# Splitting the weight panels of the latent-attention and grouped-query layers on ScalarE and VectorE instead of GpSimd

## What is computed

```python
def trunk_layer(l, x, cond, ctx):
    mod = (jax.nn.silu(cond) @ w_mod[l] + b_mod[l]).reshape(cond.shape[0], 6, D_MODEL)[:, :, None, :]
    h = rmsnorm(x, g_norm1[l]) * (1.0 + mod[:, 1]) + mod[:, 0]
    out, ctx_tensors = token_mixer(l, h, ctx)      # 0: MLA, 1: differential, 2: GQA, 3: RG-LRU
    x = x + mod[:, 2] * out
    h = rmsnorm(x, g_norm2[l]) * (1.0 + mod[:, 4]) + mod[:, 3]
    x = x + mod[:, 5] * swiglu(h, w_ffn_in[l], w_ffn_out[l])
    return x, ctx_tensors
```

## Time and profile before

| what | value |
|---|---|
| median of 3 runs | 3607.74 us (3607.37 to 3613.88) |
| the profiled execution's own time | 3609.12 us |
| its span, first to last instruction | 3606.8 us |
| mean granted TensorE clock, as a share of full speed | 0.963 |
| instructions | 52935 |

### The profile page before, as it was taken

How to read it: one execution, slowest core, us unless ns; L and a number is a source line. 1 busy time by engine, 2 the same in 40 slices (tenths; PEclk the granted TensorE clock), 3 DMA queues, 4 the chain that set the end, 5 groups by cost and what they waited for, 6 DMA issues and landing times.

```text
span 3606.8 us, 52935 instructions
## 1 busy us (share of the span) xinstructions
PE 3318.1 (92%) x20320; PEld 3011.4 (83%) x20320; DVE 1878.0 (52%) x2728; ACT 1132.7 (31%) x1742; POOL 117.5 (3%) x72
## 2 busy tenths in 40 slices
PE   7979898999998998899999788989999897899999
PEld 2556677999987776789999766779999897899999
DVE  2133346858354666466763544567573688533333
ACT  1334433211125555232111333232111377321111
POOL 0311100000000000000000221000000000000000
PEclk9989999999999999899999899999999999999999
DMA  7300013444221110153532210143432221222222
GB/s 260 109 21 13 18 33 120 145 146 142 74 82 37 42 47 17 47 176 120 177 93 70 57 31 18 35 145 124 162 123 76 62 67 47 59 76 76 76 74 77
DMA packets 421861, 304.11 MB, mean 84 GB/s; under 512 B 12019, under 2 KB 389494, under 8 KB 421622
## 3 DMA queue, kind: packets, MB, share of 16 engines
q1 hardware_dynamic: 411412, 293.23, 26.2%
q10 hardware_dynamic: 10338, 9.41, 0.8%
HBM read 298.49 MB, written 4.10 MB: 84 GB/s over the span
## 4 chain that ended last, share of the span: by engine, by line
PE 83%; DVE 7%; ACT 5%; DVEq 2%; issue 2%; ACTq 1%; DMA 1%; SPq 0%
PE psB L310 29%; PE psA L310 29%; PE psD L310 7%; PE psC L373 3%; PE psA L354 2%; PE psC L326 2%; PE psC L365 2%; PE psB L354 2%; ACT h_hi L1392 1%; PE psA L761 1%; ACT work L1389 1%; PE psB L761 1%; ACTq L1391 1%; ACT work L412 1%; DMA raw<-in_w_ffn_in 1%
## 5 line engine op out<-in xcount | busy, mean ns | idle before, releaser
L1410 ACT ACTIVATE w_hi<-raw 128x1024 fp32r<-128x1024 f32 (+1 forms) x309 | 319.3, 1035 | 1165.2 <-PE psB L310 766.2
L1943 DVE TENSOR_TENSOR w_lo<-raw,w_hi 128x1024 fp32r<-128x1024 f32 (+1 forms) x309 | 367.9, 1192 | 347.8 <-ACT w_hi L1410 347.5
L310 PE MATMUL psA<-h_hi,w_hi 128*128 128x320 f32 x1616 | 384.5, 320 | 72.0 <-DVE h_lo L2014 59.9
L310 PE MATMUL psB<-h_hi,w_hi 128*128 128x320 f32 x1616 | 370.0, 310 | 15.5 <-DVE w_lo L2296 15.5
L310 PE MATMUL psA<-h_lo,w_hi 128*128 128x320 f32 x1616 | 375.4, 314 | 0.0
L310 PE MATMUL psA<-h_hi,w_lo 128*128 128x320 f32 x1616 | 375.1, 314 | 0.0
L310 PE MATMUL psB<-h_lo,w_hi 128*128 128x320 f32 x1616 | 369.2, 310 | 0.0
L310 PE MATMUL psB<-h_hi,w_lo 128*128 128x320 f32 x1616 | 369.1, 310 | 0.0
L310 PEld LDWEIGHTS psA<-h_hi,w_hi 128*128 128x128 f32 x1616 | 273.9, 192 | 91.9 <-issue 43.8
L1973 DVE SCALAR_TENSOR_TENSOR work<-work,silu_c 128x1024 f32<-128x1024 f32 x252 | 312.5, 1281 | 12.4 <-issue 0.9
L310 PEld LDWEIGHTS psB<-h_hi,w_hi 128*128 128x128 f32 x1616 | 271.0, 188 | 17.1 <-DVE w_lo L2296 17.1
(11 more groups left out here) (290 smaller groups left out, 5137.8 us busy)
## 6 DMA issues: line engine op xcount, KB each, us to landing
raw<-in_w_ffn_in SPq DMA_DIRECT2D x176, 512.0 KB, 3.9
work<-in_w_mod SPq DMA_DIRECT2D x144, 512.0 KB, 4.8
raw<-in_w_ffn_out SPq DMA_DIRECT2D x64, 512.0 KB, 3.9
work<-in_w_mod SPq DMA_DIRECT2D x12, 2048.0 KB, 7.9
raw<-in_w_ffn_out SPq DMA_DIRECT2D x32, 384.0 KB, 3.3
raw<-in_diff_w_in SPq DMA_DIRECT2D x24, 512.0 KB, 3.8
raw<-in_lru_w_in SPq DMA_DIRECT2D x16, 512.0 KB, 4.0
raw<-in_gqa_w_in SPq DMA_DIRECT2D x12, 512.0 KB, 3.8
```

Of the source, the lines that this page charges most:

```text
L310: last = nc.tensor.matmul(out[:, b, 0:half], w[slot][:, kt * cols + c0:kt * cols + c0 + P], r[:, o:o + half], start=(kt == 0 and p == 0), ...
L1410: nc.scalar.activation(w_hi[s][:, 0:n], raw[s][:, 0:n], ACT.Copy).then_inc(hi_done, 1)
L1943: nc.vector.tensor_tensor(w_lo[s_][:, 0:n], raw[s_][:, 0:n], w_hi[s_][:, 0:n].bitcast(F32), ALU.subtract).then_inc(split_done, 1)
```

## The change

The four phases are marked dense, so that ScalarE and VectorE split their panels too. GpSimd's block and its semaphore go. The new splits are placed by hand in the programs of ScalarE and VectorE; `per=1` is for `gqa`, where a head takes one panel and the slots alternate. Nothing in TensorE's and SyncE's programs is edited.

```diff
-            add("mla_in", 3, (0, 1), [(KT, P)] * 2)
-            add("mla", HEADS, (0, 1), [(3, 192), (2, 256)])
+            add("mla_in", 3, (0, 1), [(KT, P)] * 2, True)
+            add("mla", HEADS, (0, 1), [(3, 192), (2, 256)], True)
...
-            add("gqa_kv", 2, (0, 1), [(KT, P)] * 2)
-            add("gqa", HEADS // 2, (0, 1), [(KT, P)] * 2)
+            add("gqa_kv", 2, (0, 1), [(KT, P)] * 2, True)
+            add("gqa", HEADS // 2, (0, 1), [(KT, P)] * 2, True)
...
-        @block.gpsimd
-        def _(pool):
...
         @block.scalar
...
+            for j in range(2):
+                high_part("mla_in", 0, j)
             for layer in range(DEPTH):
                 norm(2 * layer)
...
                         acts.mark(evacuate(mla_raw[t], mla_sq[t], psum[t % 2], TH), f"m{t}")
+                        if t < 4:
+                            high_part("mla_in", t // 2 + 1, t % 2)
+                        else:
+                            high_part("mla", 0, t % 2)
...
                         act_pt(act, A, h, 3, m_PT, m_PTp)
+                        if later:
+                            high_part_of_head("mla", n.next(), 0)
                         prep(evv)
                         act_pt(act, A, h, 4, m_PT, m_PTp)
+                        if later:
+                            high_part_of_head("mla", n.next(), 1)
                         prep(values)
...
-                    for step in (evqn, evqr, rsqn, rsqr, evkn, rskn, evv, values):
+                    for step in (evqn, evqr, rsqn, rsqr, evkn, rskn, evv):
                         step(h0)
+                    for j in range(2):
+                        high_part_of_head("mla", Head(0, 1), j)
+                    values(h0)
...
                         acts.mark(evacuate(gk_t[j][:, 0:T], gsq, psA, TH), "evk")
+                        high_part(("gqa_kv", "gqa")[j], 1 - j, 0)
                         g_panel("gqa_kv", j, 1)
                         acts.mark(nc.scalar.activation(halves(gvt, TH), psB[:, :, 0:TH], ACT.Copy), "evv")
+                        high_part(("gqa_kv", "gqa")[j], 1 - j, 1)
...
                         act_pt(act, A, h, 0, g_PT, g_PTp)
+                        if later:
+                            high_part_of_head("gqa", n.next(), 0, 1)
                         act_exp(act, A, h, 2, 1, scale, g_probs, g_stats)
...
-                    projected(f"out{layer}.{ch}", f"in{layer}.{ch + 1}" if ch < 2 else {0: "diff", 2: "lru"}.get(layer))
+                    projected(f"out{layer}.{ch}", f"in{layer}.{ch + 1}" if ch < 2 else {0: "diff", 1: "gqa_kv", 2: "lru"}.get(layer))
...
         @block.vector
...
+            for j in range(2):
+                low_part("mla_in", 0, j)
             for layer in range(DEPTH):
                 norm(2 * layer)
...
                     nc.vector.memset(kr_cache, 0.0).then_inc(kr_cleared, 1)
+                    for t in range(4):
+                        low_part("mla_in", t // 2 + 1, t % 2)
+                    for j in range(2):
+                        low_part("mla", 0, j)
...
                         pv.wait(dve, "pv", h)
                         out.mark(split_head(dve, h.at(T, 0)), "o")
+                        if later:
+                            low_part_of_head("mla", n.next(), 0)
                         if more:
                             probs(n, 1)
+                        if later:
+                            low_part_of_head("mla", n.next(), 1)
...
                         step(h0)
+                    for j in range(2):
+                        low_part_of_head("mla", Head(0, 1), j)
                     largest(h0, 0)
...
                     for j in range(2):
+                        low_part(("gqa_kv", "gqa")[j], 1 - j, 0)
+                        low_part(("gqa_kv", "gqa")[j], 1 - j, 1)
                         acts.wait(dve, "rsk", j)
...
                             kind(h, t)
+                            if later and (kind, t) == (probs, 2):
+                                low_part_of_head("gqa", n.next(), h.k % 2, 1)
...
-                                   f"in{layer}.{ch + 1}" if ch < 2 else {0: "diff", 2: "lru"}.get(layer), mod,
+                                   f"in{layer}.{ch + 1}" if ch < 2 else {0: "diff", 1: "gqa_kv", 2: "lru"}.get(layer), mod,
```

More of the change, by code:

```diff
@@ L1408, in high_part, with high_part_of_head @@
                 act.wait_ge(raw_in[s], i * 16 + 16 * (ph.landed[s] + 1))
-                act.wait_ge(gemm_done, i * ph.n + (ph.first + j + 1 - ph.n))
+                if ph.first or not isinstance(i, int) or i:
+                    act.wait_ge(gemm_done, i * ph.n + (ph.first + j + 1 - ph.n))
                 nc.scalar.activation(w_hi[s][:, 0:n], raw[s][:, 0:n], ACT.Copy).then_inc(hi_done, 1)
-            def high_part_of_head(name, h, j):
+            def high_part_of_head(name, h, j, per=None):
                 ph = phases[name]
-                s, n = ph.slots[j], ph.shape[j][0] * ph.shape[j][1]
-                act.wait_ge(raw_in[s], h.at(16, 16 * (ph.landed[s] + 1)))
-                act.wait_ge(gemm_done, h.at(ph.n, ph.first + j + 1 - ph.n))
+                per = per or ph.n
+                if per == 1:
+                    j = h.k % 2
+                    s, n = ph.slots[j], ph.shape[j][0] * ph.shape[j][1]
+                    act.wait_ge(raw_in[s], h.i * 16 + 16 * (ph.landed[s] + 1 + h.k // 2))
+                    act.wait_ge(gemm_done, h.at(1, ph.first + 1 - ph.n))
+                else:
+                    s, n = ph.slots[j], ph.shape[j][0] * ph.shape[j][1]
+                    act.wait_ge(raw_in[s], h.at(16, 16 * (ph.landed[s] + 1)))
+                    act.wait_ge(gemm_done, h.at(ph.n, ph.first + j + 1 - ph.n))
                 nc.scalar.activation(w_hi[s][:, 0:n], raw[s][:, 0:n], ACT.Copy).then_inc(hi_done, 1)
@@ L1504, in exp, with head @@
                         act_exp(act, A, h, t, 1, scale, m_probs, m_stats)
-                    def head(h, more):
+                    def head(h, more, later=True):
                         n = h.next()
@@ L1537, in _ @@
                     for k in range(2):
-                        head(Head(HEADS // 2 - 1, k), k == 0)
+                        head(Head(HEADS // 2 - 1, k), k == 0, later=False)
                 elif layer == 1:
```

5 lines of the change are left out of this document (2 added, 3 removed).

## The result

The changed kernel takes 3621.91 us (median of 6 runs, 3617.38 to 3628.37) against 3607.60 us for the kernel before (6 runs, 3607.28 to 3613.88): 14.3 us or 0.41% slower, ratio 1.0041 with the 95% interval 1.0029 to 1.0053. The profiled execution took 3624.09 us with a span of 3622.2 us, 15.0 us above the profiled execution of before.

The account below looks back on a forecast made before the run. TensorE, busy 92% of the span, was taken as the bound, so only its waits count. 18.5 + 7.2 + 0.1 - 3.7 - 1.7 - 1.0 + 0.3 = +19.7 us, on the median 3627.4 us; range 3614 to 3638.

Parts of the forecast that it names:

- The stall: Layer 0 head handover: TensorE's gqn waits for the w_lo behind split_head, 3.08 us in six heads, +18.5 us.
- The clock: Layer 0 heads: TensorE runs at half clock behind most of the six stalls, 1.2 us each, +7.2 us.
- rival (a): Layer 0: the stall comes, but the clock does not follow or wins its loss back; +12.5 us, 3620 us, chance 0.22.
- The forecast's own sign: Layer 0: if TensorE waits for w_lo but the head grows by 3.1 us or less, only the clock term is wrong.
- Start of layer 2: Last sum of squares and TensorE's wait shorten without GpSimd's w_lo beside them, as in layer 1; -3.7 us, lower end 2.5.
- Key and value heads: Layer 2, twice: L451 speeds up without GpSimd, less a delay by ScalarE's new w_hi; net 0.8 each, -1.7 us.
- Query heads: Layer 2: L442 falls from 1.05 to about 0.55 us without GpSimd; five heads, -1.0 us.
- some 0.2 us a head reach TensorE: Layer 2 query heads: the part of L442's saving that shortens TensorE's time; five heads, -1.0 us.
- Rival (b): Layer 2 query heads: w_hi before tile 2's exponential delays TensorE, six heads lose 1.06 each, +6.4; 3635 us, chance 0.12.
- Start of the kernel: ScalarE gets two w_hi, 2.1 us, into 1.74 us of idle before the first reciprocal root; +0.3 us.
- Rival (c): Handover in layer 0 costs nothing and only the gains remain, -6.0 us; 3602 us, chance 0.05.
- Rival (d): Whole kernel: the change doesn't do what it says, as if only the idle's place changes; within 5 us of 3608, chance 0.03.

Follow-up runs that it names:

- experiment 1: The changed kernel with the first w_lo of a latent-attention head written before VectorE waits for the head's output; 3598.05 us against 3603.59 for the kernel before.
- experiment 2: The changed kernel with that w_lo before the output only in every second head, leaving three of six stalls; 3606.25 us against 3603.59 for the kernel before.
- experiment 8: The kernel before, all splits on GpSimd, with TensorE also waiting for VectorE's split_head before gqn; 3622.50 us against 3607.01 for the kernel before.
- experiment 9: Kernel 1 with the w_lo of layer 2's query heads put behind split_head; 3606.77 us against 3605.79 for the kernel before.
- kernel 1: The changed kernel with the first latent-attention w_lo before VectorE's wait for the output; 3598.05 us against 3603.59, later 3598.80 against 3605.79, for the kernel before.
- Experiment 7: The kernel before, with GpSimd waiting for the last sum of squares before splitting layer 2's first panels; 3606.49 us against 3607.01 for the kernel before.
- the layer-0 part alone: The change for layer 0 only, GpSimd still splitting layer 2's panels; 3629.95 us against 3607.01 for the kernel before.
- The layer-2 part alone: The change for layer 2 only, GpSimd still splitting layer 0's panels; 3598.02 us against 3607.01 for the kernel before.
- experiment 10: Kernel 1 run once more, unedited, beside the kernel before; 3598.80 us against 3605.79.
- experiment 6: The layer-2 part alone: GpSimd still splits layer 0's panels; 3598.02 us against 3607.01 for the kernel before.

## Why the prediction was right, and by what it missed

The forecast was slower, 3627 us with a range of 3614 to 3638; measured were 3621.9. The mechanism was right, and one term of the sum was much too large. On the forecast's own terms, in the profiled pair, +19.7 was expected and +15.0 came.

- **The stall**: 3.08 us by six heads, 18.5. Measured 18.4, at the six places named. Its parts held to 0.1 us: `split_head` through 2.3 us after the start of `gqn` of before, a `w_lo` of 0.75, a wake-up of 0.05. Experiments 1, 2, 8 and 9 show that this is the cause.
- **The clock**: +7.2 was foretold, and this is the step that failed. The cost of the new half-clock stretches was nearly right, 7.8 us behind five stalls. Left out of the middle value was that the stretches which five of the heads had before would go with the new spacing: -6.7. The text had allowed for it only as an end of the range, a gain of 3. Net +1.1. The outcome is rival (a), which gave 3620 us and 0.22. The forecast's own sign (a head that grows by 3.1 us or less) does not catch it: a head grew from 37.3 to 40.6 us where a new stretch replaced an old one.
  The Trainium skill (TensorE: Matmul & The Clock Gate, Part 1) puts the fall of the clock down to an idle stretch before it. Five of the six stalls agree; behind the third, of 2.82 us, the clock stays full. The stretches of the kernel before agree less well: in the 7.1 us in front of one of them TensorE's longest idle time is 1.70 us. A sum that adds only what a new idle does to the clock is one-sided.
- **Start of layer 2**: -3.7 foretold, -2.6 in the profile after. The wait fell as foretold (5.70 to 3.04 us); the sums stayed at half clock, the lower end. In kernel 1 they ran at full clock and the step gave -3.8, so the size depends on the clock. Experiment 7 confirms the collision as cause of the wait. The Trainium skill (SBUF — State Buffer, Who interferes with whom) calls the shared port pair an exclusive lock for a whole instruction; the rows of experiment 7 agree: VectorE ends 0.68 us after GpSimd. The prediction misread its own rows here: the two durations of 2.80 us in the earlier trace rows do not end together, VectorE's ends 0.68 us later.
- **Key and value heads**: -1.7 foretold, -1.1 net: 2.0 by the two waits, 0.9 by matmuls behind the second that ran at full clock, and 1.9 lost again where the half-clock stretch then fell, in the first query matmuls. The wait was put at 0.8 and gave 1.0; the middle value had left the clock out.
- **Query heads**: -1.0 foretold, nothing came. The step that failed is "some 0.2 us a head reach TensorE": it followed the transposes and not the next wait behind them, which is for ScalarE's exponential. What the table shows for the stage is clock: the 1.9 just named, and -3.3 in its last two heads. Rival (b), a loss by the new `w_hi`, did not happen.
- **Start of the kernel**: +0.3 foretold, +0.4 measured. Kernel 1, which starts in the same way, has 0.0 and +0.2 at this point, so the term is not told from the scatter.
- **The rest**: +1.2 in layer 1, -3.3 in the last query heads and +1.3 behind layer 2, which no term had: -0.8 together. The second profile of the changed kernel has -0.2 behind layer 2, and the layer-0 part alone -0.6 in layer 1, whose code is the same; so these are not shown to be the change's. That the terms left out nearly cancel each other is luck.

Rival (c), that the gains are all that remains, was wrong for this kernel and is what kernel 1 shows once the stall is removed: it was foretold at 3602 us, six below, and kernel 1 measured 5.5 and 7.0 below. Rival (d) is out by the rows of the waits.

How much of kernel 1's gain is the removal of GpSimd? By its waits it is 4.7 us: 2.7 at the start of layer 2 and 1.0 at each key and value head, in every profile in which GpSimd no longer splits there. Over the whole of layer 2 kernel 1 gains 5.0 and 5.2 us (table), clock included. Another 6.7 us come in the heads of layer 0 in both of its profiles, where TensorE's idle time has not changed. They are not in every run: the profiled executions lie 14.3 and 12.7 us below that of the kernel before, the medians 5.5 and 7.0. The layer-2 part alone, with the heads of layer 0 as before, measured no less a gain. Open is whether kernel 1 keeps the clock up in layer 0: with its code there the profiles have no, no and one half-clock stretch (experiments 1, 10, 9), with the code of before five, three and three (before, experiments 6, 7). That suggests it and does not show it, and no run here says by what.

## What to carry to other kernels

When work moves from an idle engine to a busy one, look at what the consumer's queue has first after each handover: an instruction of 0.75 us placed behind a wait for the consumer itself cost 3.1 us each time, and none of it when put into the idle time in front of that wait. Follow a saved half microsecond to the next wait but one before counting it. A split that never delays anyone as a producer can still cost its neighbour through what both read, and moving it in time may only move the collision.

## What the runs showed that was not expected

- The kernel before itself varies by up to 19 us over all its runs (3594.7 to 3613.9 us), with the same program. The profiles that differ without a change in waits differ by half-clock stretches: over the heads of layer 0 the same TensorE work took 6.7 us less in the two profiles of kernel 1 than in the profile of before, at a granted clock of 1.00 against 0.96. For differences under 0.3%, one profile of each kernel is not enough.
- In the kernel before, half-clock stretches repeat once in each of five heads behind small waits (first pair: 3.52 us busy of 7.1). They start at 298.3, 335.8, 373.3, 410.9 and 448.4 us, 37.5 us apart, and a head takes 37.3. The three waits in front of the second (1.70, 1.04 and 0.85 us) are there in kernel 1 with the same lengths, and no half clock follows. So the lengths of the waits alone do not decide it.
- Six more stalls of 3 us left the mean granted clock of the heads at 0.96.
